# A hybrid encoder block's attention: pieces turned as halves of 64 partitions, another order of steps on TensorE, the causal mask inside VectorE's scan

## The chip, the cores and the metric

The kernel runs on one core of a Trainium2 chip. The metric is the device time of one execution in microseconds (us). Three runs of the kernel before stand below, and one more execution was taken by the hardware profiler; the page and all rows come from that one.

## The reference, cut to what matters

The program computes one layer of an encoder block for 2,048 tokens of width 1,024: a projection, eight heads of stick-breaking attention beside eight heads of RWKV-7 time mixing, an output projection, and a mixture of 32 experts. The change touches the attention alone:

```
for blk in range(S // Q_BLOCK):                       # 16 blocks of 128 queries
    z = einsum('bhtd,bhsd->bhts', q[t0:end], k[:end]) * scale
    causal = s_idx < t_idx
    log_keep = where(causal, log_sigmoid(-z), 0.0)
    suffix = cumsum(log_keep, axis=3, reverse=True)
    after = suffix of the next key (0 at the last)
    weights = where(causal, exp(log_sigmoid(z) + after), 0.0)
    out = einsum('bhts,bhsd->bhtd', weights, v[:end])
```

With keep = sigmoid(-z), and 1 where a key isn't visible, a running product of keep from the last key backwards gives what is left of the stick; the weight of a key is the difference of two neighbours of that product. The kernel sums by parts: it multiplies the product itself with differences of neighbouring rows of v.

## The kernel before, in words

Queries and keys lie with the head's channels on partitions, two heads (a pair) on 128 partitions. There are 4 pairs. For each pair and each block t of 128 queries the keys are worked in chunks of 512 from the last to the first; the first chunk (c == 0) holds the diagonal and is 128, 256, 384 or 512 keys wide (t % 4), the others are 512. Such a chunk, for both heads, is a step: 40 per pair, 160 in all, numbered n. Of the 40 steps of a pair 28 are 512 wide, and four each 128, 256 and 384. The class `Sticks` (L519) makes the list. Every engine walks through it in an order written out by hand; waits on semaphores tie the engines together.

A step goes through these hands:

- TensorE `scores(n)`, L618: for each head a product of 64 contraction rows (64 x 128 queries against 64 x w keys) into the two PSUM banks of `z_ps[n % 2]`.
- ScalarE `keeps(n)`, L665: sigmoid of both heads at once, 128 x 2w, into `keep`, three buffers.
- GpSimd `mask(n)`, L691, for c == 0 only: an affine select puts 1 where a key of the diagonal block isn't visible, both heads in one instruction.
- VectorE `scan(n, h)`, L713: running product from the last key to the first, one instruction per head, with the product of the chunk before as its start. Output `prod`, three buffers.
- TensorE `turn(n, h)`, L629: transposes the w/128 blocks of 128 x 128, into one PSUM bank per head.
- ScalarE `copy_turned(n, h)`, L671: one copy per head from PSUM into `prodT`, two buffers.
- TensorE `weigh(n)`, L644: for each block and head 128 keys against 64 channels of differences of v, into 64 partitions of `o_ps`.
- VectorE `add_last`, L721, once per four blocks t (a group): adds the last term out of PSUM; SyncE then stores the group and loads a later pair's q, k and v.

TensorE's order is scores(n + 2), turn(n, 0), turn(n, 1), weigh(n - 1). Its three kinds of product use three tile shapes of the array, as the rows write them: 64*128 (scores), 128*128 (turn), 128*64 (weigh). ScalarE's order is keeps(n + 2), copy(n, 0), copy(n, 1). GpSimd also computes `differences(pair)` (L685), 128 x 2048 elements, one in front and the others in the middle of the pair before. In the stretch ahead of the attention TensorE is busy with the projection (L445), while GpSimd makes masks for the time mixing.

All buffers of the attention are slices of a few large tensors: in rows, `ps` is any PSUM bank, `high` and `h_all` hold q, k, v, `keep`, `prod`, `prodT` and the output, `ident` the identity of the transposes, and after the change `low` also the constant `no_key`.

Of the kernel before, what the change touches and what calls it, by code (L numbers as in the profile page):

```python
# [20 lines left out]
ALU = mybir.AluOpType  # L21
# [3 lines left out]
P = 128  # L25
# [3 lines left out]
HD = 64  # L29
# [62 lines left out]
class Front:  # L92
# [5 lines left out]
    def __init__(self, nc, ctx, program, high, ps):  # L98
# [21 lines left out]
        self.v, self.v_before = [[h[:, x * SEQ:(x + 1) * SEQ].rearrange("p (n c) -> p n c", c=P) for h in homes] for x in (2, 3)]  # L120
        self.v_last = sb("v_last", [P, 2, NT])
        self.rest = h_flat[:, 4 * SEQ:8 * SEQ]

# [239 lines left out]
def project_channels(nc, ctx, program, front, w_in, rw_shift_mu, pT_dram, rec, load_first_pair):  # L363
# [117 lines left out]

    def on_gpsimd(pool):
        rec.make_masks(pool)

# [65 lines left out]
def stick_breaking(nc, ctx, program, front, qT_dram, kT_dram, v_dram, mixT_dram, rec, rec_inputs, mix):  # L550
# [13 lines left out]
    prod = front.rest[:, KEPT * 2 * CH:2 * KEPT * 2 * CH].rearrange("p (b h t) -> p b h t", b=KEPT, t=CH)  # L564
    prodT = front.rest[:, 4 * KEPT * CH:4 * KEPT * CH + 4 * CH].rearrange("p (b h t) -> p b h t", b=2, t=CH)
    oT_sb = front.high[:, 4 * SEQ:4 * SEQ + 2 * CH].rearrange("p (b t) -> p b t", t=CH)
    z_ps = [front.ps[:, 2 * i:2 * i + 2, :] for i in range(2)]
    prodT_ps = [front.ps[:, 4 + h, :] for h in range(2)]
    o_ps = [front.ps[:, 6 + i, :] for i in range(2)]
# [4 lines left out]
    kept = sem("p3_kept")  # L574
    masked = sem("p3_masked")
    scanned = sem("p3_scanned")
# [31 lines left out]
    def on_tensor(pe):  # L608
# [13 lines left out]
        def turn(n, h):  # L622
            w = steps[n][4]
            if n == 0:
                pe.wait_ge(front.channels_copied, CREDIT + NCH * NG)
            pe.wait_ge(scanned, CREDIT + 2 * n + h + 1)
            pe.wait_ge(turned_copied, CREDIT + 2 * n + h - 1)
            for b in range(w // P):
                last = pe.transpose(prodT_ps[h][:, b * P:(b + 1) * P], prod[:, n % KEPT, h, b * P:(b + 1) * P], ident[:, :])  # L629
            last.then_inc(turned, 1)  # L630

        def weigh(n):
# [4 lines left out]
            if c == 0 and t % 4 == 0:  # L637
                pe.wait_ge(o_ready, CREDIT + g - 1)
            pe.wait_ge(turned_copied, CREDIT + 2 * n + 2)
            blocks = w // P  # L640
            for b in range(blocks):
                for h in range(2):
                    hs = slice(h * HD, (h + 1) * HD)
                    done = pe.matmul(o_ps[g % 2][hs, t % 4 * P:(t % 4 + 1) * P], v_diff[pair % 2][:, start // P + b, hs],  # L644
                                     prodT[:, n % 2, h, b * P:(b + 1) * P],
                                     start=(c == b == 0), stop=(last_chunk and b == blocks - 1))
# [3 lines left out]
        scores(1)  # L650
        for n in range(N):
            if n + 2 < N:
                scores(n + 2)
            for h in range(2):
                turn(n, h)
            if n >= 1:
                weigh(n - 1)
        weigh(N - 1)

    def on_scalar(act):  # L660
# [5 lines left out]

        def copy_turned(n, h):
            w = steps[n][4]
            act.wait_ge(turned, CREDIT + 2 * n + h + 1)
            act.wait_ge(weighed, CREDIT + n - 1)  # L670
            act.copy(prodT[:, n % 2, h, 0:w], prodT_ps[h][:, 0:w]).then_inc(turned_copied, 1)  # L671

        keeps(0)
        keeps(1)
        for n in range(N):
            if n + 2 < N:
                keeps(n + 2)
            for h in range(2):
                copy_turned(n, h)

    def on_gpsimd(pool):
# [4 lines left out]

        def mask(n):
            w = steps[n][4]
            diag = keep[:, n % KEPT, :, w - P:w]
            pool.wait_ge(kept, CREDIT + n + 1)  # L690
            pool.affine_select(out=diag, in_=diag, compare_op=ALU.is_gt, fill=1.0, base=0,  # L691
                               pattern=[[0, 2], [-1, P]], channel_multiplier=1).then_inc(masked, 1)

        differences(0)
        for n in range(N):
            if steps[n][2] == 0:
                mask(n)
            if n % EACH == EACH // 2 and n + EACH < N:
                differences(n // EACH + 1)

    def on_vector(dve, rest_mixed):
        def scan(n, h):
            _, _, c, _, w, _ = steps[n]
            if c == 0:
                dve.wait_ge(masked, plan.unit(n) + 1)
                dve.wait_ge(scanned, CREDIT + 2 * n + h - 3)
            else:
                dve.wait_ge(kept, CREDIT + n + 1)
                dve.wait_ge(scanned, CREDIT + 2 * n + h - 1)
            dve.wait_ge(turned, CREDIT + 2 * n + h - 5)  # L710
            rows = keep[:, n % KEPT, h, 0:w][:, ::-1]
            so_far = 1.0 if c == 0 else prod[:, (n - 1) % KEPT, h, 0:1]
            dve.tensor_tensor_scan(prod[:, n % KEPT, h, 0:w][:, ::-1], rows, rows, so_far, ALU.mult, ALU.bypass).then_inc(scanned, 1)  # L713

# [1719 lines left out]
```

## Time and profile before

| | |
|---|---|
| three runs | 2821.13, 2829.88, 2831.11 us; median 2829.88 |
| profiled execution | span 2822.0 us (first to last instruction); the page gives no other time for it |
| TensorE, VectorE, ScalarE, GpSimd busy | 2654.8, 1234.4, 879.4, 848.3 us |
| attention, first scores to last `add_last` | 739.56 to 1181.92 us |

How to read it: PE is TensorE's matmuls, PEld its weight loads, DVE VectorE, ACT ScalarE, POOL GpSimd. Ends of matmuls are modelled and matmuls overlap, so a busy PE isn't PE at its peak. One `matmul` of the program in fp32 leaves two loads and two matmuls in the records, a transpose one of each. In a row, a name before and after `<-` says what is written and what is read; `x8` says how many instructions were merged; brackets hold the idle time of the engine before them and what ended it.

### The profile page before, as it was taken

Reading aid. Unit: us, or ns where it says so; the run is one execution under the profiler, and the core shown is the slowest. Engines: PE = TensorE matmul, PEld = TensorE weight load, DVE = VectorE, ACT = ScalarE, POOL = GpSimd, SP = SyncE. Lnnn points to the kernel's source line nnn. Section 1 sums busy time; section 2 is a strip of 40 time slices with the busy share of each in tenths; the row PEclk is TensorE's granted clock in tenths of the full one; section 3 lists DMA queues with packets and bytes.
Section 4 is the critical chain, followed back from the end, with each engine's and each line's share of the span. In section 5 each row is a group of like instructions: output and inputs, shape, how many; then the busy total and the mean of one; then the engine's idle time right before and its main releaser. Section 6 shows DMA issues by size and latency. Waiting matters only on the chain. (4 is left out here: it accounts for less than half of the span.)

```text
span 2822.0 us, 85417 instructions
## 1 busy us (share of the span) xinstructions
PE 2654.8 (94%) x35920; PEld 1628.8 (58%) x35921; DVE 1234.4 (44%) x2519; ACT 879.4 (31%) x1767; POOL 848.3 (30%) x978
## 2 busy tenths in 40 slices
PE   8999999999999999878888888999799999999998
PEld 3444444444466666567777775555456666666665
DVE  2333322121588887667666662343522222223222
ACT  1112110000366666645555543343311111111111
POOL 0000130000011010166655551111244444444544
PEclk9999999999999999989999999999799999999999
DMA  4111231111302203011111100754179999899994
GB/s 139 56 56 60 63 112 64 47 67 45 100 9 72 72 9 101 15 30 42 42 38 44 54 24 26 244 187 155 53 257 327 302 332 305 289 318 347 312 333 96
DMA packets 241144, 369.90 MB, mean 131 GB/s; under 512 B 35009, under 2 KB 134849, under 8 KB 238242
## 3 DMA queue, kind: packets, MB, share of 16 engines
q1 hardware_dynamic: 213186, 328.72, 33.7%
q0 software_dynamic: 27744, 38.03, 6.3%
q8 instruction: 170, 2.79, 0.4%
q14 instruction: 44, 0.36, 0.0%
HBM read 296.17 MB, written 70.52 MB: 130 GB/s over the span
## 5 line engine op out<-in xcount | busy, mean ns | idle before, releaser
L713 DVE TENSOR_TENSOR_SCAN h_all<-h_all 128x512 f32<-128x512 f32 (+3 forms) x320 | 345.7, 1129 | 69.1 <-ACT h_all L665 42.9
L2274 PE MATMUL gu_ps<-gate_up_,xT 128*32 128x256 f32 x6336 | 360.9, 379 | 5.1 <-issue 3.7
L345 PE MATMUL ps<-low,high 128*128 128x512 f32 x768 | 337.7, 596 | 2.4 <-issue 2.4
L2274 PEld LDWEIGHTS gu_ps<-gate_up_,xT 128*32 128x32 f32 x6336 | 211.0, 110 | 141.0 <-issue 14.7
L2343 DVE STREAM_TRANSPOSE xT<-xg 128x256 f32<-128x256 f32 x145 | 95.6, 660 | 442.8 <-PE gu_ps L2274 439.2
L2283 PE MATMUL y_ps<-down_,hT 128*32 128x256 f32 x4608 | 275.7, 379 | 0.6 <-ACT y L2322 0.6
L691 POOL TENSOR_SCALAR_AFFINE_SELECT h_all<-h_all 128x256 f32<-128x256 f32 x64 | 39.8, 622 | 703.5 <-ACT h_all L665 703.3
L2234 POOL DMA_INDIRECT xg<-h,take x146 | 144.4, 989 | 352.7 <-DVE h L2357 334.6
L345 PEld LDWEIGHTS ps<-low,high 128*128 128x128 f32 x768 | 144.6, 192 | 173.4 <-issue 173.4
L2242 POOL DMA_INDIRECT out<-y,put x144 | 227.0, 1577 | 57.8 <-issue 53.4
L1713 PE MATMUL ps<-high 128*128 128x512 f32 x512 | 230.7, 601 | 7.9 <-DMA high<-mixT 7.6
L2283 PEld LDWEIGHTS y_ps<-down_,hT 128*32 128x32 f32 x4608 | 155.3, 110 | 94.2 <-ACT y L2322 1.1
L445 PE MATMUL ps<-h_all,w_first 128*128 128x512 f32 x448 | 193.6, 592 | 0.0
L665 ACT ACTIVATE h_all<-ps 128x1024 f32<-128x1024 f32 (+3 forms) x160 | 143.7, 899 | 151.6 <-PE ps L618 151.5
L629 PEld LDWEIGHTS ps<-ident,h_all 128*128 128x128 f32 x1088 | 116.0, 141 | 106.9 <-DVE h_all L713 76.6
L2328 ACT ACTIVATE sil<-gu_ps 128x128 f32<-128x128 f32 x144 | 40.0, 278 | 437.9 <-PE gu_ps L2274 437.9
L445 PE MATMUL ps<-h_all,low 128*128 128x512 f32 x384 | 165.8, 592 | 0.0
L2274 PE MATMUL gu_ps<-high,xT 128*32 128x256 f32 x2880 | 163.9, 379 | 0.0
L1713 PEld LDWEIGHTS ps<-high 128*128 128x128 f32 x512 | 94.9, 192 | 113.6 <-issue 112.8
L629 PE MATMUL ps<-ident,h_all 128*128 128x128 f32 x1088 | 154.8, 281 | 4.6 <-DVE h_all L713 4.1
L494 DVE TENSOR_TENSOR low<-low 128x2048 f32<-128x2048 f32 x13 | 29.8, 2292 | 292.9 <-ACT low L471 292.9
L671 ACT COPY h_all<-ps 128x512 f32<-128x512 f32 (+3 forms) x320 | 151.0, 527 | 6.9 <-PE ps L629 6.3
(318 smaller groups left out, 4161.2 us busy)
## 6 DMA issues: line engine op xcount, KB each, us to landing
down_<-in_w_exp_down SPq DMA_DIRECT2D x128, 512.0 KB
gate_up_<-in_w_exp_gate SPq DMA_DIRECT2D x88, 512.0 KB
gate_up_<-in_w_exp_up SPq DMA_DIRECT2D x88, 512.0 KB
high<-in_w_exp_gate SPq DMA_DIRECT2D x40, 512.0 KB
high<-in_w_exp_up SPq DMA_DIRECT2D x40, 512.0 KB
pT<-low SPq DMA_DIRECT2D x13, 1024.0 KB, 3.9
rkv<-pT SPq DMA_DIRECT2D x96, 128.0 KB, 2.5
high<-in_x SPq DMA_DIRECT2D x16, 512.0 KB, 4.1
```

The lines of the kernel that those rows point to most:

```text
L345: done = pe.matmul(qkv_ps[:, part, :], hT[:, s, k, :], w_sb[:, k, part * SBW:(part + 1) * SBW], start=(k == 0), stop=(k == KT - 1))
L445: last = pe.matmul(p_ps[:, s, g, :], w[s][:, k, :], h_all[:, k, g * GT:(g + 1) * GT], start=(k == 0), stop=(k == KT - 1))
L629: last = pe.transpose(prodT_ps[h][:, b * P:(b + 1) * P], prod[:, n % KEPT, h, b * P:(b + 1) * P], ident[:, :])
L665: act.activation(keep[:, n % KEPT, :, 0:w], z_ps[n % 2][:, :, 0:w], ACT.Sigmoid, scale=-SCALE).then_inc(kept, 1)
L671: act.copy(prodT[:, n % 2, h, 0:w], prodT_ps[h][:, 0:w]).then_inc(turned_copied, 1)
L713: dve.tensor_tensor_scan(prod[:, n % KEPT, h, 0:w][:, ::-1], rows, rows, so_far, ALU.mult, ALU.bypass).then_inc(scanned, 1)
L1713: done = pe.matmul(self.ps[:, s, half, :], self.rows[:, s, k, :], self.w[:, k, half * 512:(half + 1) * 512], start=(k == 0), stop=(k == KT ...
L2234: pool.indirect_dma_start(out=xg[j][:, :], out_offset=None, in_=h2_quarters[:, :], in_offset=bass.IndirectOffsetOnAxis(ap=take[j][:, 0:1], ...
L2242: pool.indirect_dma_start(out=out_quarters[:, :], out_offset=bass.IndirectOffsetOnAxis(ap=put[j][:, 0:1], axis=0), in_=y[j][:, :], in_offs ...
L2274: last = pe.matmul(gu_ps[QUARTERS[q], 0:2 * P].rearrange("t (x f) -> t x f", x=2), xT[:, k * ROWS:(k + 1) * ROWS], w_gu[s][:, k, :, q * P: ...
L2283: last = pe.matmul(y_ps[QUARTERS[q], 0:256], hT[:, k * ROWS:(k + 1) * ROWS], w_d[s][:, k, q * 256:(q + 1) * 256], start=(k == 0), stop=(k ...
L2343: dve.transpose(xT[:, :].rearrange("p (k t) -> p k t", k=KT), xg[j][:, :].rearrange("t (p k) -> t k p", k=KT))
```

## The change

Four things change, all in the attention.

1. `turn(n, h)` transposes each 128 x 128 block as two halves of 64 partitions (64 queries), with the 64 x 64 corner of the identity, in the tile shape 64*128 that the scores use. Half f = 0 of both heads goes to one PSUM bank, half f = 1 to the other. One semaphore increment per step, not per head.
2. `copy_turned(n)` copies both banks of a step in one instruction, in runs of 64 elements, into `prodT[n % 3]`, now three buffers with the halves interleaved again.
3. TensorE's order, for two steps a and a + 1: turn(a), scores(a + 2), scores(a + 3), turn(a + 1), weigh(a - 1), weigh(a). ScalarE's: copy(a), keeps(a + 2), keeps(a + 3), copy(a + 1).
4. The mask leaves GpSimd. A constant `no_key` (0, and 1 where a key of the diagonal block isn't visible) is made once, and the first scan of a block takes `max` with it; the other scans stay as they are. `differences` of all pairs stand one behind the other on GpSimd, each waiting for its v. `add_last` of a group comes one step later in VectorE's order.

The core of the diff:

```diff
     def on_gpsimd(pool):
+        pool.wait_ge(front.projected, NT * 3)
+        pool.memset(front.no_key, 0.0)
+        pool.drain()
+        pool.affine_select(out=front.no_key[:, 512 - P:512], in_=front.no_key[:, 512 - P:512], compare_op=ALU.is_gt, fill=1.0, base=0,
+                           pattern=[[-1, P]], channel_multiplier=1).then_inc(front.no_key_ready, 1)
         rec.make_masks(pool)
...
             pe.wait_ge(scanned, CREDIT + 2 * n + h + 1)
-            pe.wait_ge(turned_copied, CREDIT + 2 * n + h - 1)
+            pe.wait_ge(turned_copied, CREDIT + n)
             for b in range(w // P):
-                last = pe.transpose(prodT_ps[h][:, b * P:(b + 1) * P], prod[:, n % KEPT, h, b * P:(b + 1) * P], ident[:, :])
-            last.then_inc(turned, 1)
+                for f in range(2):
+                    rows, x = slice(f * HD, (f + 1) * HD), (h * (w // P) + b) * HD
+                    last = pe.transpose(prodT_ps[:, f, x:x + HD], prod[rows, n % KEPT, h, b * P:(b + 1) * P], ident[rows, rows])
+            if h == 1:
+                last.then_inc(turned, 1)
...
-        for n in range(N):
-            if n + 2 < N:
-                scores(n + 2)
+        for a in range(0, N, 2):
             for h in range(2):
-                turn(n, h)
-            if n >= 1:
-                weigh(n - 1)
+                turn(a, h)
+            for n in (a + 2, a + 3):
+                if n < N:
+                    scores(n)
+            for h in range(2):
+                turn(a + 1, h)
+            if a >= 1:
+                weigh(a - 1)
+            weigh(a)
         weigh(N - 1)
...
-        def copy_turned(n, h):
+        def copy_turned(n):
             w = steps[n][4]
-            act.wait_ge(turned, CREDIT + 2 * n + h + 1)
-            act.wait_ge(weighed, CREDIT + n - 1)
-            act.copy(prodT[:, n % 2, h, 0:w], prodT_ps[h][:, 0:w]).then_inc(turned_copied, 1)
+            act.wait_ge(turned, CREDIT + n + 1)
+            act.wait_ge(weighed, CREDIT + n - 2)
+            act.copy(prodT[n % 3][:, 0:2 * w].rearrange("p (x f t) -> p f x t", f=2, t=HD),
+                     prodT_ps[:, :, 0:w].rearrange("p f (x t) -> p f x t", t=HD)).then_inc(turned_copied, 1)
...
-        differences(0)
-        for n in range(N):
-            if steps[n][2] == 0:
-                mask(n)
-            if n % EACH == EACH // 2 and n + EACH < N:
-                differences(n // EACH + 1)
+        for pair in range(PAIRS):
+            differences(pair)
...
+            dve.wait_ge(kept, CREDIT + n + 1)
...
+            if c == 0:
+                if n == 0:
+                    dve.wait_ge(front.no_key_ready, 1)
+                scan = dve.tensor_tensor_scan(out, rows, no_key[:, CH - w:CH][:, ::-1], 1.0, ALU.mult, ALU.max)
+            else:
+                scan = dve.tensor_tensor_scan(out, rows, rows, prod[:, (n - 1) % KEPT, h, 0:1], ALU.mult, ALU.bypass)
+            scan.then_inc(scanned, 1)
...
-            if n >= 2 and plan.closes_group(n - 2):
-                add_last(n - 2)
+            if n >= 3 and plan.closes_group(n - 3):
+                add_last(n - 3)
```

How the order moves is seen best on TensorE, in the first pair at steps 14 to 18 (widths 512, 256, 512, 384, 512). Before: L618 is scores (from those of step 16 on), L629 turn (from step 14 on), L644 weigh.

```order
L618 MATMUL ps<-high 128x512 x2
L629 MATMUL ps<-ident,h_all 128x128 x8
L644 MATMUL ps<-h_all,high 64x128 x8
L618 MATMUL ps<-high 128x512 x2
L629 MATMUL ps<-ident,h_all 128x128 x4
L644 MATMUL ps<-h_all,high 64x128 x8
L618 MATMUL ps<-high 128x384 x2
L629 MATMUL ps<-ident,h_all 128x128 x8
L644 MATMUL ps<-h_all,high 64x128 x4
```

The three kinds of product alternate step by step, and each neighbour has another tile shape.

The same place after the change, beginning with the turn of step 14; L638 is turn, L625 scores, L654 weigh, and shapes are those of the output.

```order
L638 MATMUL ps<-ident,h_all 128x64 x16
L625 MATMUL ps<-high 128x512 x4
L638 MATMUL ps<-ident,h_all 128x64 x8
L654 MATMUL ps<-h_all,high 64x128 x8
L654 MATMUL ps<-high 64x128 x8
L638 MATMUL ps<-ident,h_all 128x64 x16
L625 MATMUL ps<-high 128x384 x2
L625 MATMUL ps<-high 128x512 x2
L638 MATMUL ps<-ident,h_all 128x64 x16
L654 MATMUL ps<-h_all,high 64x128 x12
```

Turns have twice as many, narrower transposes; turn, two scores and turn stand together, and the weighings of two steps behind one another.

ScalarE at the same place. Before, L665 is keeps (from that of step 16 on) and L671 a copy per head:

```order
L665 ACTIVATE h_all<-ps 128x1024
L671 COPY h_all<-ps 128x512 x2
L665 ACTIVATE h_all<-ps 128x1024
L671 COPY h_all<-ps 128x256 x2
L665 ACTIVATE h_all<-ps 128x2x384
```

After, L679 is keeps and L685 the copy of a step, beginning with the copy of step 14:

```order
L685 COPY h_all<-ps 128x2x8x64
L679 ACTIVATE h_all<-ps 128x1024 x2
L685 COPY h_all<-ps 128x2x4x64
L685 COPY h_all<-ps 128x2x8x64
L679 ACTIVATE h_all<-ps 128x2x384
```

Two keeps now stand together, and so do the copies of steps a + 1 and a + 2.

## Rows read from the trace of the kernel before

**Rows 1.** The page, section 1: busy us (share of the span) and instructions.
```profile
PE 2654.8 (94%) x35920; PEld 1628.8 (58%) x35921; DVE 1234.4 (44%) x2519; ACT 879.4 (31%) x1767; POOL 848.3 (30%) x978
```

**Rows 2.** Windows: us, busy (x instructions) per engine, granted clock, DMA share, GB/s.
```profile
739.56:1181.92 442.36, 436.03 (x3908) 279.62 (x3904) 355.98 (x337) 282.31 (x482) 53.27 (x67) 1.00 0.19 55
```

**Rows 3.** Timeline, 1015 to 1023 us: start, us, engine, line, op, names, shapes [idle].
```profile
1015.90 0.30 PEld L618 LDWEIGHTS ps<-high 64*128 64x128 f32 x4 [0.17 <-issue]
...
1016.39 4.69 DVE L713 TENSOR_TENSOR_SCAN h_all<-h_all 128x512 f32<-128x512 f32 x4 [0.24 <-POOL h_all L691]
1016.96 0.86 PEld L629 LDWEIGHTS ps<-ident,h_all 128*128 128x128 f32 x8 [0.76 <-DVE h_all L713]
...
1017.98 0.85 PEld L644 LDWEIGHTS ps<-h_all,high 128*64 128x64 f32 x16 [0.17 <-issue]
...
1019.01 0.30 PEld L618 LDWEIGHTS ps<-high 64*128 64x128 f32 x4 [0.17 <-issue]
...
1020.18 1.03 ACT L665 ACTIVATE h_all<-ps 128x1024 f32<-128x1024 f32 x1 [1.12 <-PE ps L618]
...
1021.11 1.07 ACT L671 COPY h_all<-ps 128x512 f32<-128x512 f32 x2
1021.24 2.46 DVE L713 TENSOR_TENSOR_SCAN h_all<-h_all 128x512 f32<-128x512 f32 x2 [0.16 <-ACT h_all L665]
1022.11 0.30 PEld L618 LDWEIGHTS ps<-high 64*128 64x128 f32 x4 [0.17 <-issue]
...
1022.53 0.85 PEld L629 LDWEIGHTS ps<-ident,h_all 128*128 128x128 f32 x8
```

**Rows 4.** Timeline: the first scores, the first scans, the last two weighings.
```profile
739.56 0.52 PEld L618 LDWEIGHTS ps<-high 64*128 64x128 f32 x8 [0.84 <-issue]
...
742.65 2.06 DVE L713 TENSOR_TENSOR_SCAN h_all<-h_all 128x128 f32<-128x128 f32 x4 [4.58 <-POOL h_all L691]
...
1179.85 1.73 PEld L644 LDWEIGHTS ps<-h_all 128*64 128x64 f32 x32 [0.17 <-issue]
```

**Rows 5.** Weight loads by form (busy us, mean ns | idle), and a run of them in time.
```profile
L345 PEld LDWEIGHTS ps<-low,high 128*128 128x128 f32 x768 | 144.6, 192 | 173.4 <-issue 173.4
L629 PEld LDWEIGHTS ps<-ident,h_all 128*128 128x128 f32 x1088 | 116.0, 141 | 106.9 <-DVE h_all L713 76.6 <-issue 28.9
L644 PEld LDWEIGHTS ps<-h_all 128*64 128x64 f32 x1088 | 57.8, 136 | 13.2 <-issue 13.2
...
1832.33 1.87 PEld L1927 LDWEIGHTS ps<-w_r,h2T 128*128 128x128 f32 x16
```

**Rows 6.** Windows, TensorE alone, in the time mixing: PE busy (x records), clock, DMA.
```profile
1356.50:1357.00 0.50, 0.50 (x52) 1.00 0.24 78
```

**Rows 7.** VectorE's scans: two forms, and two narrow scans in time.
```profile
L713 DVE TENSOR_TENSOR_SCAN h_all<-h_all 128x512 f32<-128x512 f32 x224 | 273.6, 1266 | 52.6 <-ACT h_all L665 42.9 <-POOL h_all L691 9.6
L1203 DVE TENSOR_TENSOR_SCAN Lsum<-chunk_reset,sig 128x512 f32<-128x512 f32 x16 | 20.5, 1279 | 30.9 <-ACT sig L1075 30.9
...
768.36 0.74 DVE L713 TENSOR_TENSOR_SCAN h_all<-h_all 128x128 f32<-128x128 f32 x2 [0.24 <-POOL h_all L691]
```

**Rows 8.** Waits for GpSimd (us, times, longest), and GpSimd's differences in time.
```profile
DVE h_all L713 <- POOL h_all L691: 26.2, 44, 4.6
...
784.44 4.52 POOL L685 TENSOR_TENSOR h_all<-h_all 128x2048 f32<-128x2048 f32 x1
...
789.82 0.31 PEld L629 LDWEIGHTS ps<-ident,h_all 128*128 128x128 f32 x3 [1.82 <-DVE h_all L713]
```

**Rows 9.** A turn and the copy that waits for it; ScalarE's narrowest activation.
```profile
766.74 0.86 PEld L629 LDWEIGHTS ps<-ident,h_all 128*128 128x128 f32 x8
...
767.43 1.07 ACT L671 COPY h_all<-ps 128x512 f32<-128x512 f32 x2 [0.19 <-PE ps L629]
...
L665 ACT ACTIVATE h_all<-ps 128x256 f32<-128x256 f32 x16 | 6.3, 393 | 4.4 <-PE ps L618 4.4
```

**Rows 10.** `add_last` by form.
```profile
L721 DVE TENSOR_TENSOR high<-ps,v_last 128x512 f32<-128x512 f32 x16 | 11.0, 689 | 18.7 <-issue 18.7
```

More of the change, by code:

```diff
@@ L564, in stick_breaking @@
     prod = front.rest[:, KEPT * 2 * CH:2 * KEPT * 2 * CH].rearrange("p (b h t) -> p b h t", b=KEPT, t=CH)
-    prodT = front.rest[:, 4 * KEPT * CH:4 * KEPT * CH + 4 * CH].rearrange("p (b h t) -> p b h t", b=2, t=CH)
+    prodT = [front.rest[:, (4 * KEPT + 2 * b) * CH:(4 * KEPT + 2 * b + 2) * CH] for b in range(2)] + [front.high[:, 4 * SEQ + 2 * CH:4 * SEQ + 4 * CH]]
     oT_sb = front.high[:, 4 * SEQ:4 * SEQ + 2 * CH].rearrange("p (b t) -> p b t", t=CH)
     z_ps = [front.ps[:, 2 * i:2 * i + 2, :] for i in range(2)]
-    prodT_ps = [front.ps[:, 4 + h, :] for h in range(2)]
+    prodT_ps = front.ps[:, 4:6, :]
+    no_key = front.no_key
     o_ps = [front.ps[:, 6 + i, :] for i in range(2)]
@@ L665, in keeps @@
             act.activation(keep[:, n % KEPT, :, 0:w], z_ps[n % 2][:, :, 0:w], ACT.Sigmoid, scale=-SCALE).then_inc(kept, 1)
-        def copy_turned(n, h):
+        def copy_turned(n):
             w = steps[n][4]
-            act.wait_ge(turned, CREDIT + 2 * n + h + 1)
-            act.wait_ge(weighed, CREDIT + n - 1)
-            act.copy(prodT[:, n % 2, h, 0:w], prodT_ps[h][:, 0:w]).then_inc(turned_copied, 1)
+            act.wait_ge(turned, CREDIT + n + 1)
+            act.wait_ge(weighed, CREDIT + n - 2)
+            act.copy(prodT[n % 3][:, 0:2 * w].rearrange("p (x f t) -> p f x t", f=2, t=HD),
+                     prodT_ps[:, :, 0:w].rearrange("p f (x t) -> p f x t", t=HD)).then_inc(turned_copied, 1)
         keeps(0)
         keeps(1)
-        for n in range(N):
[L676 to L679, printed above, removed]
+        for a in range(0, N, 2):
+            copy_turned(a)
+            for n in (a + 2, a + 3):
+                if n < N:
+                    keeps(n)
+            copy_turned(a + 1)
     def on_gpsimd(pool):
@@ L703, in scan @@
             _, _, c, _, w, _ = steps[n]
+            dve.wait_ge(kept, CREDIT + n + 1)
             if c == 0:
-                dve.wait_ge(masked, plan.unit(n) + 1)
                 dve.wait_ge(scanned, CREDIT + 2 * n + h - 3)
             else:
-                dve.wait_ge(kept, CREDIT + n + 1)
                 dve.wait_ge(scanned, CREDIT + 2 * n + h - 1)
-            dve.wait_ge(turned, CREDIT + 2 * n + h - 5)
+            dve.wait_ge(turned, CREDIT + n - 2)
             rows = keep[:, n % KEPT, h, 0:w][:, ::-1]
-            so_far = 1.0 if c == 0 else prod[:, (n - 1) % KEPT, h, 0:1]
-            dve.tensor_tensor_scan(prod[:, n % KEPT, h, 0:w][:, ::-1], rows, rows, so_far, ALU.mult, ALU.bypass).then_inc(scanned, 1)
+            out = prod[:, n % KEPT, h, 0:w][:, ::-1]
+            if c == 0:
[5 more added lines that the diff above has]
+            scan.then_inc(scanned, 1)
         def add_last(n):
```

14 lines of the change are left out of this document (4 added, 10 removed).

## The prediction

> **What bounds the kernel now.** I read the busy shares first. TensorE is busy for 94% of the span [rows 1], which says little about one stage, so I went to the stretch that the change touches: from the first scores at 739.56 us to the last `add_last` at 1181.92 us, 442.4 us. In it TensorE counts 436.0 us of work, VectorE 356.0, ScalarE 282.3 and GpSimd 53.3, at a granted clock of 1.00, the 2.4 GHz level [rows 2].
>
> Then the timeline of wide steps (512 keys) [rows 3]. TensorE goes round scores, turn, weigh: scores at 1015.90, turn at 1016.96, weigh at 1017.98, next scores at 1019.01, next again at 1022.11. That is 3.1 us a step and no gap that another engine causes. Scores stream for 0.86 us, and each of the three phases takes 1.02 to 1.06: about 0.85 of streaming and 0.17 to 0.2 before the first weight load of the next phase. A scores phase of 128 keys takes 0.42 (1022.11 to 1022.53): a quarter of 0.85, and again 0.2. So a phase costs 0.85 u + 0.18, where u is the width over 512. A pair of heads has 40 steps with widths that sum to 34 u: 3 x (34 x 0.853 + 40 x 0.18) = 108.6 us, four pairs 434.6; with something over 1 us for each of three stalls (below) and some 4 us of start and end that is the stretch. TensorE's order of work bounds this stretch; VectorE's scans (2.46 us for the two of a wide step [rows 3]) wait for it.
>
> The 0.18 is paid where the tile shape changes. Where two phases of one shape follow each other it is absent: two weighings in a row, 32 loads, take 1.73 us from the first load to the end of the last, 16 x 0.107 and nothing more; the first two scores' eight loads take 0.52 us [rows 4].
>
> **The change, part by part.**
>
> *Order.* Two steps had six shape changes and will have two (into the weighings and out of them). Per pair of heads 120 x 0.18 = 21.6 us become 40 x 0.18 = 7.2: 14.4 us off TensorE, 58 us over four pairs.
>
> *Turning by halves.* A wide step has 8 transposes of 128 x 128 in 0.853 us, 107 ns each. It will have 16 of 64 x 128, each streaming 64 columns, two row halves side by side. What must be known is whether halves overlap and what a load costs. Overlap: scores use this tile shape, and their eight loads in 0.52 us are four pairs of 0.107 plus one latency of 0.09; one after the other they would be 0.94 [rows 4]. Load: ordinary loads of 64 and 128 columns last 136 and 192 ns, 0.87 ns a column; a transpose's load of 128 columns lasts 141, so it costs like 64 columns, about 57 ns [rows 5]. A stream of 128-column ordinary loads with 36-column matmuls goes at 1.87/16 = 0.117 us each [rows 5]: there the load binds. And TensorE started up to 52 records in 0.5 us later on [rows 6], so 27 ns a record is not too dense. Eight pairs at 54 ns: 0.43 us; eight pairs at 107 ns: 0.86. I take 0.43, since the only row of a transpose's load says 57 ns, and keep 0.86 as the other end. For the sum alone each transpose pair is worth 0.42 x 34 x 4 = 57 us of TensorE's time between the ends, but below 0.86 other engines take over (next).
>
> The Trainium skill ("TensorE: Matmul & The Clock Gate", section on LDWEIGHTS) gives a load as its columns over 1.2 GHz, with the contraction rows without effect. The ordinary loads of this trace agree; the transpose's 141 ns does not. By the rule halves would load for 107 ns and the turn would stay at 0.86 us: the first rival below.
>
> *Copy.* ScalarE's two copies of a wide step (1.07 us) become one of 1,024 elements. The activation of 1,024 elements lasts 1.03 and the next instruction starts 0.92 after it [rows 3]. I take 0.93 from start to start. That it writes runs of 64 elements no row prices; from -0.1 to +0.2 us.
>
> *Mask.* GpSimd's 64 selects go; VectorE waited 26.2 us for them in total, 44 times [rows 8]. TensorE was the bound, so most of that was cover, but in the new order the latency would count, and it is gone. The first scan of a unit now reads a second tensor and uses max. A scan with two different tensors and an add lasts 1,279 ns against 1,266 [rows 7]: nothing, up to +0.02 us each. The constant is made once in TensorE-bound projection: nothing.
>
> *GpSimd's differences.* They come earlier, but there are still three in the stretch, each holding up the scan that it meets: 4.52 us on GpSimd at 784.44, after which TensorE's weight loads sat idle for 1.82 us ahead of a turn [rows 8] where 0.76 is usual [rows 3]. Before, VectorE's slack swallowed the rest. With VectorE and the chain nearly the bound it will cost most of its 4.5: I take 4 each, 12 us in three.
>
> **What is late next.** TensorE needs 34 x (0.853 + 0.43 + 0.853) + 7.2 = 79.8 us a pair; VectorE at full density, 4.69 us for four wide scans [rows 3], about 84. So a chain decides. From the end E of scan (a,1), a wide: 0.1 to the turn; 8 transposes of head 1 and their latency, 0.5 (before: 0.69 from the first load to the copy for four [rows 9], less 3 x 0.107 - 7 x 0.027 and 0.05 for shorter streams); copy 0.93; keeps 1.03; 0.03 to scan (a+2): E + 2.6. VectorE itself is through with step a+1 at E + 2.3. Then the two scans, 2.46: 5.07 us for two wide steps, 6.22 before.
>
> For other widths the same with ScalarE's 0.39 us for 2 x 128 [rows 9], scans of 0.74 for 128 [rows 7], and lines between. Let me write (w_a, w_a+2), each with the wider of chain and VectorE, plus the scans of a+2: (512,512) 5.07 four times; (384,512) 4.80 three times; (128,512) and (256,512) 4.75 three; (512,384) 4.24 twice; (256,384) 4.14; (512 or 384,128) 3.03 four; (512 or 128,256) 3.6 twice; (128,384) 3.45. Sum 84.3 us a pair. TensorE's order adds to it: where a+2 is narrow, both weighings of 0.85 stand ahead of its turn, which starts at E + 4.65 (2.4 for scan (a+1,1), 0.23, 0.17, 1.71, 0.17) though its scan is done earlier. After VectorE's own work this costs 1.1 us three times, 0.3, 0.85, and 0.43 twice: 5.3. `add_last` (0.69 [rows 10]) stands in VectorE's way in three of four: 2.1. So 91.7 a pair, 366.8, and 12 for the differences: 379. The stretch begins with 3.1 us up to scan 0 [rows 4] and its 0.74 and ends, after the last even step's E, with scan 159, its turn and three weighings in a row (2.4 + 0.43 + 0.17 + 2.56 + 0.2 = 5.75) where the sum has 3.03 for a next step: 3.8 + 379 + 2.7 = 385.5 against 442.4, 57 us less. I keep 2 for small waits that I haven't counted, and take 55.
>
> The profiled execution's span is 2822.0 us, 7.9 under the median of the runs; I take the difference off the median: 2829.9 - 55 = **2775**. What follows the stretch starts when it ends; the loads for it are issued from group 11 on, some 90 us ahead still.
>
> **Rivals.**
>
> 1. *The turn stays at 0.86 us*, since the load takes 107 ns or the halves do not overlap at 54 ns each. For it: the skill's rule, and no row with a half transpose. Against: 141 ns and the scores' loads. TensorE 34 x 2.56 + 7.2 = 94 a pair, 3 for waits behind narrow steps, so 389, plus 6 for differences and 7 for the ends: 402, 40 less: **2790**.
>
> 2. *The chain through ScalarE is longer than I have it*: the merged copy starts only when both heads are turned, and each wide two steps go through copy, keeps, two scans in series. If strided copy, PSUM and semaphores add 0.8 us per two steps (80 of them, nearly all on the chain), 55 becomes less by 40 or so: **2815**. Against: the parts are all read from rows.
>
> 3. *Slower*: the halves are turned one after the other with 107 ns each, since their loads or bank writes exclude each other in transpose form. Then a wide turn is 1.71, TensorE 34 x 3.42 + 7.2 = 123.5 us a pair, 494 + 8 = 502: **2890**. It decides from 1.2 us a wide turn on, 150 ns a pair of halves: (108.6 - 3 - 7.2)/34 - 1.71. Against: the scores' loads in pairs [rows 4].
>
> 4. *The change doesn't do what it says*: the 0.18 is not the shape but the dependence, and stays. Then with 0.43 for the turn TensorE has 34 x 2.14 + 21 = 94, as in 1.
>
> **How the numbers follow.** Forecast (2775, own range 2762 to 2789) 0.55; rivals 1 and 4 0.25; rival 2 0.12; no change 0.03; slower 0.05. If VectorE ran without any gap the stretch would be about 355 and the time 2743, which I hold unlikely. The range of 8 in 10 goes from 2760 to 2808. About 0.5% (14 us) is what a measurement of this kernel can tell from nothing: faster 0.92, same 0.03, slower 0.05.
>
> **What would show it.** In the profile of the changed kernel: the stretch 385 us long; 16 loads of a wide turn in 0.45 to 0.5 us (0.9 is rival 1, 1.7 rival 3); the 0.17 gap twice per two steps; wide double steps every 5.1 us; scans waiting for `keeps` for 0.3 us after odd steps and about 2 us after narrow even ones; scans of 1.26 us with the mask; three stalls of 4 us. Wrong would be wide double steps above 5.6, or a granted clock below 1.00 in the stretch.

## The result, and the profile after

The changed kernel takes 2781.99 us (median of four runs, 2779.84 to 2788.61); the kernel before, with the runs made beside it, 2830.49. The ratio is 0.9847, interval [0.9822, 0.9872]: 1.5% faster, 48.5 us by the medians. The profiled execution took 2779.84 us, its span is 2778.0, 44.0 less than before.

The page, section 1, and the window from the first scores' weight load to the last `add_last`. They answer to [rows 1] and [rows 2].

```profile
PE 2580.4 (93%) x37008; PEld 1612.3 (58%) x37009; DVE 1217.8 (44%) x2519; ACT 866.9 (31%) x1607; POOL 811.2 (29%) x916
```

```profile
739.69:1135.42 395.73, 361.19 (x4996) 262.18 (x4992) 344.89 (x337) 270.23 (x322) 16.46 (x3) 0.98 0.21 62
```

The stretch is 395.7 us long for 442.4: 46.6 less. The rest of the program takes 2.6 us more, hence the span's 44.0. From the last `add_last` to the first expert matmul it is 872.6 us before and 874.6 after, and 868.6 to 876.1 in the runs below, so that part of it, 2 us, is within what this varies. TensorE is no longer busy throughout, VectorE is now busy for 87% of the stretch (80% before), and the granted clock is 0.98 where it was 1.00.

Two wide steps in the third pair of heads, from the timeline of the changed kernel. L638 is turn, L625 scores, L654 weigh, L679 keeps, L685 copy, L720 and L722 the scan with and without the mask.

```profile
1026.12 2.34 DVE L720 TENSOR_TENSOR_SCAN h_all<-h_all,low 128x512 f32<-128x512 f32 x2 [0.19 <-ACT h_all L679]
...
1026.38 0.85 PEld L654 LDWEIGHTS ps<-high 128*64 128x64 f32 x16
...
1027.20 0.91 PEld L654 LDWEIGHTS ps<-h_all,high 128*64 128x64 f32 x16
...
1028.28 0.57 PEld L638 LDWEIGHTS ps<-ident,h_all 64*128 64x128 f32 x16 [0.17 <-issue]
...
1028.38 2.43 DVE L722 TENSOR_TENSOR_SCAN h_all<-h_all 128x512 f32<-128x512 f32 x2
1028.77 0.31 PEld L625 LDWEIGHTS ps<-high 64*128 64x128 f32 x4
...
1029.03 1.01 ACT L685 COPY high<-ps 128x1024 f32<-128x1024 f32 x1 [1.12 <-PE ps L638]
...
1029.95 1.94 ACT L679 ACTIVATE h_all<-ps 128x1024 f32<-128x1024 f32 x2
...
1031.01 4.81 DVE L722 TENSOR_TENSOR_SCAN h_all<-h_all 128x512 f32<-128x512 f32 x4 [0.20 <-ACT h_all L679]
...
1033.16 0.69 PEld L638 LDWEIGHTS ps<-ident,h_all 64*128 64x128 f32 x16 [0.17 <-issue]
```

This answers to [rows 3]. These two wide steps take 4.89 us (1026.12 to 1031.01 on VectorE, 4.88 on TensorE), 6.2 before; at most other places two wide steps take 5.00. VectorE scans almost without a pause, 0.2 us in front of every second step. A whole turn of 16 half transposes has its loads in 0.57 us and the scores' first load follows 0.49 after the turn's first (0.43 was forecast): no gap between the two, as they share a shape. The 0.17 stands where the weighings end.

The loads of the turn by form, the answer to [rows 5]: a half transpose's load lasts as long as a whole one's did (141 ns), where an ordinary load of 128 columns lasts 192.

```profile
L638 PEld LDWEIGHTS ps<-ident,h_all 64*128 64x128 f32 x2176 | 94.6, 140 | 103.2 <-DVE h_all L722 43.6 <-issue 41.5 <-DVE h_all L720 15.7
```

Then the narrow beginning of the next pair, steps 120 (128 wide) and 122 (384), from the timeline:

```profile
1036.27 1.73 PEld L654 LDWEIGHTS ps<-h_all,high 128*64 128x64 f32 x32
...
1038.17 0.20 PEld L638 LDWEIGHTS ps<-ident,h_all 64*128 64x128 f32 x4 [0.17 <-issue]
1038.28 0.95 PEld L625 LDWEIGHTS ps<-h_all 64*128 64x128 f32 x8
...
1038.55 0.37 ACT L685 COPY h_all<-ps 128x256 f32<-128x256 f32 x1 [1.15 <-PE ps L638]
1039.26 1.88 ACT L679 ACTIVATE h_all<-ps 128x768 f32<-128x768 f32 x2 [0.34 <-PE ps L625]
...
1040.10 1.81 DVE L720 TENSOR_TENSOR_SCAN h_all<-h_all,low 128x384 f32<-128x384 f32 x2 [2.48 <-ACT h_all L679]
```

VectorE idles 2.48 us. The turn of step 120 stood behind two weighings, as forecast. But `keeps` of step 122 then waited for the scores (0.34 <-PE ps L625), not for the copy, which was over at 1038.92.

Last, one of GpSimd's differences, in the first pair, from the timeline and from windows of TensorE's granted clock (the column before the DMA share). It answers to [rows 8].

```profile
769.07 5.52 POOL L701 TENSOR_TENSOR h_all<-h_all 128x2048 f32<-128x2048 f32 x1 [356.00 <-DMA v_last<-v]
...
771.99 4.85 DVE L722 TENSOR_TENSOR_SCAN h_all<-h_all 128x512 f32<-128x512 f32 x2 [1.73 <-ACT h_all L679]
...
775.72 0.32 PEld L638 LDWEIGHTS ps<-ident,h_all 64*128 64x128 f32 x8 [2.91 <-DVE h_all L722]
```

```profile
775.00:776.00 1.00, 0.28 (x8) 0.28 (x8) 1.00 (x2) 0.00 (x0) 0.00 (x0) 1.00 0.00 0
776.00:782.00 6.00, 5.32 (x36) 2.87 (x34) 4.10 (x6) 2.88 (x3) 0.00 (x0) 0.50 0.11 44
782.00:784.00 2.00, 2.00 (x30) 1.84 (x26) 2.00 (x2) 0.65 (x2) 0.00 (x0) 0.79 0.03 8
```

Two scans that take 2.44 us elsewhere take 4.85. TensorE has nothing to do for 2.7 us, and 0.3 us after it starts again its clock falls to 0.50, the 1.2 GHz level, for 6.8 us. Single microseconds show the same at 871 to 875 and 970 to 974, after the two other differences, and at 1131 to 1135, in the tail where the last turns wait for scans. Of the kernel before, each of the 442 windows of one microsecond from 740 to 1182 us has 1.00.

### The profile page after: what moved, and what is told of

It reads as the page before. It is cut to its first block and busy times, and to the rows that moved or that the text cites. A ratio compares the mean times of both kernels' runs of the same rounds, so it can differ in the third digit from the quotient of the medians.

```text
span 2778.0 us, 87151 instructions
## 1 busy us (share of the span) xinstructions
PE 2580.4 (93%) x37008; PEld 1612.3 (58%) x37009; DVE 1217.8 (44%) x2519; ACT 866.9 (31%) x1607; POOL 811.2 (29%) x916
## 5 line engine op out<-in xcount | busy, mean ns | idle before, releaser
L722 DVE TENSOR_TENSOR_SCAN h_all<-h_all 128x512 f32<-128x512 f32 x192 | 235.3, 1275 | 28.1 <-ACT h_all L679 28.1
L638 PEld LDWEIGHTS ps<-ident,h_all 64*128 64x128 f32 x2176 | 94.6, 140 | 103.2 <-DVE h_all L722 43.6
L638 PE MATMUL ps<-ident,h_all 64*128 64x64 f32 x2176 | 115.6, 232 | 34.4 <-DVE h_all L722 12.8
L447 PEld LDWEIGHTS ps<-h_all,w_first 128*128 128x128 f32 x448 | 85.1, 190 | 106.7 <-issue 106.7
L701 POOL TENSOR_TENSOR h_all<-h_all 128x2048 f32<-128x2048 f32 x2 | 11.0, 5520 | 448.6 <-DMA v_last<-v 448.6
L679 ACT ACTIVATE h_all<-ps 128x1024 f32<-128x1024 f32 (+3 forms) x160 | 136.7, 898 | 13.7 <-PE ps L625 10.7
```

Source lines behind the costliest of these rows:

```text
L447: last = pe.matmul(p_ps[:, s, g, :], w[s][:, k, :], h_all[:, k, g * GT:(g + 1) * GT], start=(k == 0), stop=(k == KT - 1))
L638: last = pe.transpose(prodT_ps[:, f, x:x + HD], prod[rows, n % KEPT, h, b * P:(b + 1) * P], ident[rows, rows])
L679: act.activation(keep[:, n % KEPT, :, 0:w], z_ps[n % 2][:, :, 0:w], ACT.Sigmoid, scale=-SCALE).then_inc(kept, 1)
L722: scan = dve.tensor_tensor_scan(out, rows, rows, prod[:, (n - 1) % KEPT, h, 0:1], ALU.mult, ALU.bypass)
```

## The experiments

The theory: the gain comes from the tile shapes and from halves that stream side by side, after which VectorE and the chain into its next scan are the bound. What disagreed with the forecast were the length (395.7 us for a forecast of 385.5) and the clock. The stretch is the same work in every run, so its length in the trace is the sharpest measure; it goes from the first scores to the last `add_last`. The last eight runs were made on two other chips, four on each (chips 2 and 3 in the table); there the kernel before takes 2907 and 2903 us. The 73 to 76 us more lie in the expert stage (752 us on the first chip, 827 on these from its first to its last gate matmul), so times are compared by their ratio to the kernel before beside them.

| kernel | stretch, us | median, us | ratio to the kernel before |
|---|---|---|---|
| before | 442.4 | 2830.5 | 1 |
| changed | 395.7 | 2782.0 | 0.9847 [0.9822, 0.9872] |
| whole transposes, new order | 434.1 | 2821.7 | 0.9974 [0.9960, 0.9988] |
| half transposes, old order | 397.4 | 2776.6 | 0.9826 [0.9796, 0.9857] |
| whole transposes, old order | 443.8 | 2831.5 | 1.0009 [0.9993, 1.0025] |
| most differences left out | 384.9 | 2799.2 | 0.9906 [0.9890, 0.9923] |
| changed, again (chip 3) | 395.9 | 2853.4 | 0.9835 [0.9816, 0.9853] |
| differences in parts (chip 2) | 383.6 | 2837.9 | 0.9769 [0.9751, 0.9787] |
| the same, again (chip 3) | 383.8 | 2844.3 | 0.9802 [0.9784, 0.9819] |
| parts, old order (chip 2) | 386.7 | 2843.0 | 0.9783 [0.9766, 0.9799] |
| parts, mask on GpSimd (chip 3) | 397.3 | 2853.6 | 0.9832 [0.9810, 0.9854] |
| parts, half of the copy (chip 3) | 384.3 | 2838.6 | 0.9784 [0.9762, 0.9807] |
| late weighing (chip 2) | 402.6 | 2857.4 | 0.9827 [0.9811, 0.9844] |
| before, mask in the scan (chip 2) | 444.0 | 2900.8 | 0.9988 [0.9977, 0.9999] |

**Halves and order, each undone.** Three kernels show each part with and without the other. The first undoes the halves:

```diff
-                for f in range(2):
-                    rows, x = slice(f * HD, (f + 1) * HD), (h * (w // P) + b) * HD
-                    last = pe.transpose(prodT_ps[:, f, x:x + HD], prod[rows, n % KEPT, h, b * P:(b + 1) * P], ident[rows, rows])
+                last = pe.transpose(prodT_ps[:, h, b * P:(b + 1) * P], prod[:, n % KEPT, h, b * P:(b + 1) * P], ident[:, :])
```

> The changed kernel with one part undone: transposes are whole again (128 x 128, one bank per head), so turns have the tile shape 128*128; the new order, merged copy and scan mask stay. By the forecast's terms TensorE has four shape changes per two steps and 0.853 us a wide turn: 34 x 2.56 + 80 x 0.18 = 101.4 us a pair, 406, and about 415 for the stretch with its ends and differences: 2806 us, between 2800 and 2812. If the 0.18 us were owed to the dependence and not to the shape, the stretch would stay near 440 and the time near 2825. If halving is worth nothing, it would equal the changed kernel, 2782.

The second has TensorE's and ScalarE's loops of the kernel before (TensorE's is shown, cut):

```diff
-        for a in range(0, N, 2):
-            ...
+        for n in range(N):
+            if n + 2 < N:
+                scores(n + 2)
+            for h in range(2):
+                turn(n, h)
+            if n >= 1:
+                weigh(n - 1)
```

> The changed kernel with the order of before on TensorE and ScalarE (scores(n+2), turn(n), weigh(n-1); keeps(n+2), copy(n)); half transposes, merged copy, scan mask stay. Shape changes are two per step: 34 x 2.13 + 80 x 0.18 = 86.8 us a pair, 347, near VectorE's own 84 a pair and with a looser chain through ScalarE. The forecast's terms then give a stretch of 380 to 395 and 2770 to 2784 us: the order would be worth little once turns are halved. The rival, that the order carries the gain (58 us of TensorE's time by the forecast's first term), says 2800 or more.

The third has both edits.

> Both undone: order of before and whole transposes; what is left of the change is the merged copy, the scan mask and the place of the differences. TensorE 108.6 us a pair as before, so the stretch 436 to 443 and 2824 to 2831 us. If mask or copy were the cause of the gain, it would be 2800 or less.

Measured: the new order alone takes 8.3 us off the stretch (434.1), the halves alone 45.0 (397.4), both 46.6, neither nothing (443.8). The order alone was expected to bring over 20.

Part of what it fell short lies in GpSimd's differences (below), which hold up these kernels in each of the first three pairs, and not in the last: from the first scan of a pair's step 10 to that of its step 20 the kernel with the new order alone takes 28.2, 32.0 and 31.5 us, and 26.0 in the last. From its first scan to the last `add_last` the last pair takes 112.2 us before, 107.7 with the new order alone, 98.2 with the halves alone. So in an undisturbed pair the order alone brings 4.5 us, of 7.2 by the forecast's terms for whole transposes, and the halves alone 14.0.

Timeline of the kernel with whole transposes in the new order, where L636 is turn, L652 weigh, L677 keeps, L683 copy:

```profile
1023.10 0.91 PEld L652 LDWEIGHTS ps<-h_all,high 128*64 128x64 f32 x16
...
1024.18 0.20 PEld L636 LDWEIGHTS ps<-ident,h_all 128*128 128x128 f32 x2 [0.17 <-issue]
1024.55 0.30 PEld L625 LDWEIGHTS ps<-high 64*128 64x128 f32 x4 [0.17 <-issue]
...
1025.73 1.94 ACT L677 ACTIVATE h_all<-ps 128x1024 f32<-128x1024 f32 x2 [0.70 <-PE ps L625]
1026.47 0.86 PEld L636 LDWEIGHTS ps<-ident,h_all 128*128 128x128 f32 x8 [0.76 <-issue]
1026.79 2.46 DVE L719 TENSOR_TENSOR_SCAN h_all<-h_all 128x512 f32<-128x512 f32 x2 [1.89 <-ACT h_all L677]
```

The 0.17 stands at each change of shape and is absent within the pair of weighings at 1022.28 and 1023.10, 0.82 apart. Between turn and scores it stands here (1024.55), where the turn's shape is 128*128, and not in the changed kernel (1028.77), where the shapes agree and the same products follow each other: so the rival that it belongs to the dependence is out. But here VectorE idles 1.89 us. TensorE changes shape less often, but at the narrow steps that saving went into waiting: turn, scores and keeps stand in series after two weighings. In the old order, with halves, TensorE has only two changes a step and never two weighings ahead of a turn, and VectorE scans six wide times without a pause:

```profile
1020.06 7.49 DVE L716 TENSOR_TENSOR_SCAN h_all<-h_all 128x512 f32<-128x512 f32 x6 [0.74 <-ACT h_all L675]
...
1020.40 0.30 PEld L625 LDWEIGHTS ps<-high 64*128 64x128 f32 x4 [0.17 <-issue]
...
1022.85 0.30 PEld L625 LDWEIGHTS ps<-high 64*128 64x128 f32 x4 [0.17 <-issue]
```

That is 2.50 us a wide step on VectorE, as in the changed kernel (4.89 to 5.00 for two). Once turns are halved, the new order brings nothing that these runs can tell: 1.6 us of stretch for it, and in the last pair 98.2 us in the old order and 98.0 in the new (the changed kernel, again), while the medians of 2776.6 and 2782.0 lean the other way, with intervals that overlap.

**The differences.** This kernel leaves out 15 of the 16 blocks of the differences of the last three pairs:

```diff
+            part = slice(0, NT if pair == 0 else 1)
-            pool.tensor_tensor(v_diff[s], v_diff[s], v_sb[s], ALU.subtract).then_inc(v_ready, 1)
+            pool.tensor_tensor(v_diff[s][:, part, :], v_diff[s][:, part, :], v_sb[s][:, part, :], ALU.subtract).then_inc(v_ready, 1)
```

> The changed kernel, leaving out 15/16 of the differences of v of pairs 1 to 3 on GpSimd (part of the computation). In the changed kernel's trace each of them lasts 5.5 us, holds VectorE, leaves TensorE idle 2.7 us, and TensorE's clock is then granted at 0.50 for 3.8 to 6.6 us. Theory: three stalls of about 4 us, and 7 us for the clock: 15 to 19 us less, 2763 to 2767. Rival: the stall is swallowed as before the change, and the clock's dips cost nothing since TensorE has slack: 4 us or less, 2778 or more.

The stretch is 384.9 us, 10.9 less, and the clock stays at 1.00 until its tail. The time as a whole, 2799 us, says nothing here: the output differs, tokens go to other experts, and the expert stage takes longer. I hadn't thought of that when I put numbers of time on it; the first expert matmul starts 17 us earlier than in the changed kernel, at 1992.9 us.

If the collision costs that much, the same work at places where VectorE idles anyway, behind the scans of steps 13, 25, 29 and 33 of the pair before, should cost nothing (the core of the edit):

```diff
+        IDLE = {13: (0, 5), 25: (5, 10), 29: (10, 14), 33: (14, 16)}
+        differences(0)
+        for n in range(N - EACH):
+            if n % EACH in IDLE:
+                pool.wait_ge(scanned, CREDIT + 2 * n + 2)
+                differences(n // EACH + 1, *IDLE[n % EACH])
```

> The changed kernel, with the differences of pairs 1 to 3 cut into four parts of 2 to 5 blocks, each held back until a scan after which VectorE sits idle in the trace (after steps 13, 25, 29, 33 of a pair; idle 1.7, 1.3 and 0.8 us there). With most of the differences left out the attention took 384.9 us from first scores to last add, against 395.7. Theory (collision and the clock's fall that it brings cost 11 us): the granted clock stays at 1.00 inside the stretch, stretch 384 to 389, time 2771 to 2776 for 2782. Rival: the parts hold up the chain instead (16 x 0.35 us per pair just where a copy and keeps are on their way): stretch unchanged at 395.

> The changed kernel itself, beside the kernel with the differences in parts on the same chip, since chips differ in the expert stage. Ratio to the kernel before 0.984 to 0.985; stretch 395 to 396 us.

> The changed kernel with the differences in four parts at VectorE's idle places, again, beside the changed kernel. Theory: 12 us less in the stretch (383.6 against 395.7) and so a ratio to the kernel before 0.004 to 0.006 under that of the changed kernel. Rival: the lower ratio of the other call (0.977) came from that chip, and the two are alike.

Measured: 383.6 and 383.8 us on two chips, 12.1 less than the changed kernel's 395.9 on the second. All of the cost is gone with the work still done. In time, on that chip, the medians are 2844.3 and 2853.4, 9 us apart; the ratios 0.9802 and 0.9835 have intervals that just overlap, but each of its four times (2842.5 to 2846.8) lies under each of the other four (2850.7 to 2857.3). One forecast of this run failed: the clock doesn't stay at 1.00 throughout, it is at 0.50 for 6.8 us at the start (743 to 750 us). The window behind that, with the clock at 1.00:

```profile
770.00:1120.00 350.00, 325.91 (x4624) 237.14 (x4622) 307.66 (x306) 247.31 (x293) 15.12 (x12) 1.00 0.18 54
```

This version beats both kernels.

What is the price of the collision, and what that of the clock? In the last pair, which runs beside no difference, 23.7 us pass in the changed kernel from the first scan of the pair's step 10 to that of step 20. In the three pairs with one it is 28.5, 27.3 and 26.6, and in its second execution (chip 3) 28.4, 29.5 and 26.3; with the differences in parts it is 23.7 in every pair. So a difference, with the fall of the clock where one follows, costs 2.6 to 5.8 us, by where it meets the scans. The third one shows the clock's share: both executions have the same pause of TensorE's loads behind it, 2.48 us, but in the second one no fall follows (its window from 971 to 978 us, with the clock at 1.00):

```profile
971.00:978.00 7.00, 5.79 (x70) 3.96 (x72) 7.00 (x9) 3.93 (x6) 0.00 (x1) 1.00 0.02 6
```

That is 26.6 us with 3.4 us at half clock and 26.3 without: here the fall costs 0.3 us and the collision 2.6. Where TensorE's work is the bound a fall costs more. With the mask in the scan of the kernel before, one of 3.4 us (906.6 to 910.0) makes its pair 1.6 us longer than the next (112.3 and 110.7); the one in the changed kernel's tail comes with 99.7 us for the last pair, where its second execution, without it, has 98.0. The second execution has two falls for the four of the first and its stretch is as long. I take the collision for the larger part of the 12 us; the fall of 6.8 us behind the first difference can't be told from its collision, since both executions have it.

With the old order the parts do nearly as well:

> Half transposes, merged copy and scan mask with the order of before, and the differences in parts as in the other run. The old order with half transposes measured 2776.6 (stretch 397.3, as long as the changed kernel's), with the clock at half in three places after differences. Theory: 10 to 14 us less, stretch 384 to 388, time 2764 to 2768, the fastest of all so far. Rival: no gain, since this order has its idle time elsewhere (about 2777).

386.7 us, 10.6 less than with that order and whole differences (397.4). The 3.1 us to the new order aren't its price: the places were picked for the new order, and in the old one the parts meet scans (three of them take 5.14 us from 769.04 on, where 3.8 is usual). In the last pair, which has no parts, both orders take the same, as above.

**The mask.**

> The kernel before, with the mask alone moved into the scan (GpSimd's selects gone, constant and max in the first scan; differences stay in the middle of the pair before). TensorE bounds that kernel, so VectorE's 26 us of waiting for GpSimd were cover: 2826 to 2832 us, no change. Rival: the mask's latency was on the path at the narrow steps: 2815 or less.

> Differences in parts, and the mask back on GpSimd (a select per first chunk between keeps and scan, half transposes and new order stay). Theory: here VectorE and the chain are the bound, and the select's 0.4 to 0.75 us stand between keeps and scan at 64 steps; at half of them VectorE would otherwise be ready: 10 to 20 us more than with the mask in the scan, stretch 394 to 404. Rival: it is hidden as in the kernel before (there the mask alone moved the stretch from 442.4 to 444.0 us): 384 to 387.

In the kernel before, the mask in the scan changes nothing (444.0 us for 442.4, and 1.6 of that is the fall of the clock named above). In the kernel with halves, new order and differences in parts, taking it back to GpSimd costs 13.5 us (397.3 for 383.8). From that kernel's waits (us in total, times, longest):

```profile
DVE h_all L735 <- POOL h_all L710: 31.1, 48, 4.6
```

The wait is hardly longer than the 26.2 us of [rows 8], but there TensorE covered it. An edit that is worth nothing alone is worth 13.5 us once its cover is gone.

**The chain through the copy.** This kernel, which has the differences in parts, copies only one of the two banks of a turned step, so half of the weights are missing:

```diff
-            act.copy(prodT[n % 3][:, 0:2 * w].rearrange("p (x f t) -> p f x t", f=2, t=HD),
-                     prodT_ps[:, :, 0:w].rearrange("p f (x t) -> p f x t", t=HD))
+            act.copy(prodT[n % 3][:, 0:2 * w].rearrange("p (x f t) -> p f x t", f=2, t=HD)[:, 0:1],
+                     prodT_ps[:, 0:1, 0:w].rearrange("p f (x t) -> p f x t", t=HD))
```

> Differences in parts, and the copy of a turned step reduced to one of its two banks (half of prodT isn't written, so half of the weights are left out; read the attention stretch, since the expert stage depends on the data). It takes 0.45 us out of the chain turn, copy, keeps, scan. Theory (that chain decides at wide steps): VectorE's idle 0.2 to 0.5 us ahead of even wide steps goes, and 0.4 less at narrow ones: stretch 383.6 down to 372 to 377. Rival (TensorE's order or VectorE decides): 381 to 384.

384.3 us, 383.8 with the whole copy: no gain at all. My chain lacked a link. From its timeline:

```profile
1011.79 0.31 PEld L625 LDWEIGHTS ps<-high 64*128 64x128 f32 x4
...
1012.06 0.59 ACT L685 COPY h_all<-ps 128x512 f32<-128x512 f32 x1 [1.67 <-PE ps L638]
...
1012.98 1.94 ACT L679 ACTIVATE h_all<-ps 128x1024 f32<-128x1024 f32 x2 [0.33 <-PE ps L625]
...
1014.04 2.34 DVE L726 TENSOR_TENSOR_SCAN h_all<-h_all,low 128x512 f32<-128x512 f32 x2 [0.20 <-ACT h_all L679]
```

The copy now ends 0.33 us before `keeps` starts, and `keeps` starts no sooner, since the scores whose sigmoid it takes come out 1.19 us after their first load. VectorE's idle 0.20 is what it was.

**Late weighing.**

```diff
+            if late is not None:
+                weigh(late)
             for h in range(2):
                 turn(a + 1, h)
...
-            weigh(a)
+            late = a if a + 2 < N and steps[a + 2][4] <= 256 else None
+            if late is None:
+                weigh(a)
```

> The changed kernel, but where step a+2 is 256 wide or narrower, weigh(a) is put off until after turn(a+2) and the scores that follow it. The forecast has TensorE's turn of such a step late by 1.1 us three times, 0.85 and 0.3 a pair, because two weighings stand ahead of it. Putting one off frees 0.85 us and costs two more shape changes of 0.17: five places a pair, 2.5 us a pair, so 10 us less: 2772. Rival: that idle time of VectorE comes from the chain copy, keeps alone, and the extra changes cost: 2782 to 2789.

The stretch is longer, 402.6 us for 395.7; the time doesn't show it (0.9827, intervals overlap). The same narrow place in its timeline (L684 keeps, L725 scan):

```profile
1043.12 1.00 PEld L625 LDWEIGHTS ps<-h_all 64*128 64x128 f32 x8
...
1044.88 0.85 PEld L654 LDWEIGHTS ps<-h_all,high 128*64 128x64 f32 x16 [0.76 <-issue]
1044.97 1.81 DVE L725 TENSOR_TENSOR_SCAN h_all<-h_all,low 128x384 f32<-128x384 f32 x2 [1.90 <-ACT h_all L684]
1045.90 0.32 PEld L638 LDWEIGHTS ps<-ident,h_all 64*128 64x128 f32 x8 [0.17 <-issue]
```

VectorE idles 1.90 us for 2.48, about what the put-off weighing was to give. But it now stands between the scores and the turn of step a + 1. The clock fell to 0.50 in five places ahead of the tail, for three in the changed kernel; the two new ones (at 950 and 1052 us) each come with 1.6 us more in the first ten steps of their pair than the second pair has there. And the differences hold longer: from step 10 to 20 it is 27.2, 29.1 and 29.2 us with one and 23.2 without, 16 us in all where the changed kernel loses 11. Together that is 8 us, so the 7 are covered without any for the edit itself; a run of it with the differences in parts would show that, and there is none.

## Why the prediction came out right, and what in it was wrong

- **Shape changes.** The mechanism is as forecast: 0.17 us at each change, none within a shape. As a share of the gain it was over-read. 58 us of TensorE's time stood under this heading; alone it brings 8 (4.5 in the one pair that no difference disturbs), and after the halves nothing. The sum didn't add the terms, it took TensorE only until another limit came, and for that reason survived.
- **Halves.** 27 to 30 ns a half transpose: eight loads in 0.33 us, sixteen in 0.57, where 0.14 is the last load's own. That is a little over the 0.43 us taken (0.49 from the turn's first load to the scores'), and not 0.86. The first rival, 107 ns for the load, is out. That was the rule of the Trainium skill ("TensorE: Matmul & The Clock Gate", section on LDWEIGHTS: a load's columns over 1.2 GHz): the ordinary loads of this kernel agree with it, the transposes' don't.
- **Copy, mask, scan.** The copy of 1,024 elements lasts 1.02 and the next instruction starts 0.92 after it, as taken. The masking scan costs nothing: 1,206 ns, 1,275 for the others. The mask's cover was TensorE's, as said.
- **Differences.** 12 us forecast as three times 4, 12.1 measured, but the three aren't alike: 2.6 to 5.8 us each. Each lasts 5.4 to 5.5 us on GpSimd in the changed kernel, not 4.5, and the pause in TensorE's work that it makes is followed by 3.4 to 6.8 us at half clock, which the forecast didn't have. A clock below 1.00 in the stretch was named as a sign that something is wrong, and it came. That the size fits is partly luck.
- **Wide steps.** 4.89 to 5.00 us for two against 5.07.
- **The chain at narrow steps: the step that failed.** The forecast ran it through copy and keeps alone and summed 91.7 us a pair. The kernel with differences in parts, whose pairs have no collision, starts its pairs' first scans at these times (timeline):

```profile
835.00 1.87 DVE L726 TENSOR_TENSOR_SCAN h_all<-h_all,low 128x128 f32<-128x128 f32 x4
...
929.56 1.88 DVE L726 TENSOR_TENSOR_SCAN h_all<-h_all,low 128x128 f32<-128x128 f32 x4
```

94.6 us a pair (the next one too), 2.9 too much, four times: 11.6 us, the 10.2 by which the stretch was missed and a little more. After a narrow turn the copy is short (0.37 us), but the scores behind it are not: 0.64 us for 384 keys, 0.85 for 512, and 0.3 until ScalarE can start. `keeps` waited for them at 1039.26 above, and in the pair from 929.5 to 1024.1 us of the kernel with parts five times (us in total, times, longest):

```profile
ACT h_all L679 <- PE ps L625: 2.0, 5, 0.6
```

That is 2.0 us of the 2.9; the rest is open. The scores stand nowhere in the forecast's chain. At wide steps that did no harm, since they end when the copy does: `keeps` starts 1.18 us after the scores' first load (1028.77 to 1029.95), and with half a copy 1.19. At narrow steps they end last, and there the chain runs through them.
- **The sum.** 385.5 us and 2 more for small waits forecast, 395.7 measured; 55 us less forecast, 48.5 measured by the medians. Rivals 1 to 4 are out: the turn is at 0.49 us, the copy lasts what was taken, nothing runs one after the other, and the 0.17 goes with the shape. Rival 2's own price doesn't follow from its terms: 0.8 us on 80 double steps is 64 us, not 40.

## What to carry to other kernels

Where one engine bounds a loop, the terms taken off it don't add: price each against the engine that comes next, and test them one at a time in both orders. An edit that is free or cheap while the bound covers it (here the mask, the differences) must be priced again once the bound is gone. When two inputs of a step arrive together at one width, keep both in the chain for every width: the one left out can decide at another. Work on GpSimd that collides with VectorE belongs into VectorE's idle places, in parts.

## What the runs showed of the hardware

- A transpose of 64 partitions streams beside one of the other 64 at 27 to 30 ns each (eight loads in 0.33 us, sixteen in 0.57). A transpose's weight load of 128 columns lasts 140 to 141 ns, an ordinary one 192.
- Between products of two tile shapes 0.17 us pass on TensorE, and none between the same products once the shapes agree.
- TensorE's clock fell to 0.50 after its loads had paused for 2.5 to 2.9 us in the changed kernel, and stayed there for 3.4 to 6.8 us. The length of the pause doesn't decide it alone: a pause of 2.48 us in the second execution had no fall behind it; three of 1.82 us in the kernel before had none, and one of 1.86 us in that kernel with the mask in the scan had one. A fall of 3.4 us cost 0.3 us where VectorE's scans were the bound, and 1.6 to 1.7 where TensorE was.
- A difference of 2,048 elements on GpSimd lasted 4.52 us before and 4.8 to 5.5 in the two executions of the changed kernel, where it met VectorE's scans at other places. A scan that met it lasted 5.27 us before and 3.7 to 5.5 after.
- The scan that starts from a constant (first chunks, 512 wide) lasts 1,206 ns on average (1,232 in the kernel before), the one that starts from the last element of the one before 1,275. It is the start and not the `max` with a second tensor: with the mask back on GpSimd the first chunks' scans have neither and last 1,204.

```profile
L735 DVE TENSOR_TENSOR_SCAN h_all<-h_all 128x512 f32<-128x512 f32 x32 | 37.3, 1204 | 5.9 <-POOL h_all L710 5.9
```
